# Mixture of experts on one core: eight experts gathered at once, and a scatter that takes one half of the tokens per expert pair

## The chip, the cores and the metric

The kernel runs on one core of a Trainium2 chip. The core has five engines, each with its own instruction queue: TensorE (PE, matmuls; its weight loads are listed as PEld), VectorE (DVE), ScalarE (ACT), GpSimd (POOL) and SyncE (SP, which here only issues loads). They wait for each other through semaphores. The metric is the device time of one execution in microseconds (us), the median of several.

## What is computed

Two transformer blocks over 256 tokens of width 1024, all in fp32. The change touches one stage of the first block, the mixture of 32 experts, each with 256 hidden columns; every token goes to two of them:

```python
def hier_moe(h, w_rg, b_rg, w_re, b_re, w_gate, w_up, w_down):
    ...
    x_pad = jnp.zeros((P, D), h.dtype).at[dest].set(xt[stok])
    ...
    def expert_block(args):
        xb, e = args
        hid = jax.nn.silu(xb @ w_gate[e]) * (xb @ w_up[e])
        return hid @ w_down[e]
    ...
    out = jnp.zeros((T, D), jnp.float32).at[tok_pad].add(y.astype(jnp.float32) * w_pad[:, None])
    return out.astype(h.dtype).reshape(B, L, D)
```

## The kernel before

**Slots.** The 256 tokens lie in two halves (tiles j = 0, 1) of 128. Each expert has CAP = 64 slots, CT = 32 for each half. DVE writes `Pm`, a 0/1 matrix with a column for each slot, by comparing each token's position with the slot numbers (`places`, L2509, L2511); `Pw` is the same with the router's weights (L2534). If an expert has over 32 tokens of a half, the branch `over > 0` runs further rounds; for the inputs measured it is not taken, but every engine has its code and jumps over it.

**Gather.** On PE, `gather` (L1673, L1678) multiplies the normalised tokens `xn2` by `Pm`: for a block of 128 model columns k, two matmuls, one for each half. A fill is two blocks, in PSUM bank 1 or 2; ACT scales it into `xgs` (`gathered`, L989, L995). Four experts (a quad, two pairs) are gathered at once, so a fill is 4 matmuls of 128 columns, and four fills make a quad. Four fills stand ahead of the loop; in each pair two more are made for the next quad, for the last quad too, whose fills nobody uses. There are 36 fills in all.

**A pair.** PE's loop (L1697) has 4 passes of 4 pairs. For each pair, in this order: gate and up into bank 0 (L1716, 32 matmuls, two experts side by side in 64 columns each; the two weight tiles of each come from `spare` or from the ring), a gather fill, `scatter` (L1687) of the pair before, transposes of the hidden rows and of `Pw` into bank 3 (L1727, L1728), a gather fill, and down into banks 1 and 2 (L1739). Beside it ACT makes silu (L1009), its gathered rows (L995) and the copy of the transposes `hT_PT` (L1012); DVE makes the hidden rows `hid` (L2544) and multiplies the result in banks 1 and 2 by the gate row into `ysb` (L2547), one copy of 128 partitions for each bank. Rows 0 to 63 of `ysb` belong to token half 0, rows 64 to 127 to half 1; the scatter is therefore 4 matmuls of 64 rows and 512 columns, into the four banks `acc`, where the sum over all experts stands. The first pair's scatter adds zeros; `last` (L1743) makes the one of pair 15.

**Waits.** PE's gather waits for `y_taken` (DVE's copies of the pair before), the transposes for `hid_ready`, down for `t_taken` (ACT's copy of the transposes), the first pair for the last of the gathered rows.

**Weights.** A pair takes 6 tiles of 1 MB. Pairs 0, 2, 4, ... read them from `spare`, the others from the ring; the first two pairs' tiles are there when the stage begins. SP then loads the tiles of pair n + 2 into the same places, in order: two when gate of pair n is done, two after up, two after down (L589 to L595). 84 tiles are loaded so.

## Time and profile before

| what | us |
|---|---|
| median of 3 runs (lowest, highest) | 1232.71 (1231.29, 1232.84) |
| the profiled execution, its own time | 1231.89 |
| its span | 1229.6 |
| PE busy in it | 1169.0 (95%) |
| DVE busy | 408.4 (33%) |
| ACT busy | 322.3 (26%) |
| MoE stage, first gather to last scatter | 540.6 to 790.6 |

The run fetched code by two queues, 0.70 MB and 0.15 MB, and executed 16523 instructions in the span.

The profile records one execution. All times in its rows are from the start of the span; the 2.3 us between the span and the execution's own time lie around it. A matmul in fp32 shows as two records, so the counts of PE rows are twice those of the code. PE's records overlap a little at their ends: the time from one start to the next says more than the duration.

### The profile page before, as it was taken

The page shows a single profiled execution, that of the slowest core. Times are in us where ns is not written, and L with a number is a line of the kernel's source. Part 1 is how long each engine was busy: PE and PEld are TensorE (multiplying, and loading weights), DVE is VectorE, ACT ScalarE, POOL GpSimd, SP SyncE. Part 2 cuts the span into 40 slices and gives each one's busy share as a digit, 9 for nine tenths or more (in the row PEclk, how much of TensorE's full clock was granted, in tenths as well). Part 3 has the DMA queues.
Part 4 walks back from the last instruction along what each step waited for, and adds up shares of the span by engine and source line. Part 5 has one row for each costly group of instructions (what it writes and reads, how often), then busy time and mean ns, then how long its engine had stood idle before and what let it go on. Part 6 is the DMA issues. An engine that isn't in the chain of part 4 may idle for free.

```text
span 1229.6 us, 16523 instructions
## 1 busy us (share of the span) xinstructions
PE 1169.0 (95%) x6732; PEld 868.1 (71%) x6732; DVE 408.4 (33%) x1006; ACT 322.3 (26%) x739; POOL 32.2 (3%) x56
## 2 busy tenths in 40 slices
PE   7999999999999999989999999889778989999997
PEld 6788888888887778865555555467656848887443
DVE  2324334213322131231111111125886432225445
ACT  3481010053423130141122211243475241000000
POOL 0000000000000002000000000014000000000000
PEclk9999999999999999999999999999879999999999
DMA  9923113212247784629999999523200413434430
GB/s 387 405 102 137 69 69 134 106 70 103 103 146 316 281 335 155 241 88 390 410 422 425 423 415 378 206 103 136 106 1 1 171 69 139 169 137 171 171 136 34
DMA packets 34153, 241.66 MB, mean 197 GB/s; under 512 B 3898, under 2 KB 4154, under 8 KB 5804
## 3 DMA queue, kind: packets, MB, share of 16 engines
q1 hardware_dynamic: 32940, 234.46, 48.7%
q0 software_dynamic: 720, 3.12, 0.7%
q10 hardware_dynamic: 432, 3.23, 0.6%
q8 instruction: 43, 0.70, 0.2%
q14 instruction: 18, 0.15, 0.0%
HBM read 239.74 MB, written 1.05 MB: 196 GB/s over the span
## 4 chain that ended last, share of the span: by engine, by line
PE 87%; DVE 6%; ACT 3%; DMA 2%; issue 1%; SPq 0%; DVEq 0%; ACTq 0%
PE bank L1318 22%; PE bank L1345 12%; PE bank L1716 9%; PE bank L1327 8%; PE bank L2066 6%; PE bank L1739 5%; PE bank L1678 3%; PE bank L1390 3%; PE bank L1687 3%; DMA ring<-in_stream 2%; PE bank L1410 1%; PE bank L1584 1%; PE bank L1581 1%; PE bank L1529 1%; PE bank L2038 1%
## 5 line engine op out<-in xcount | busy, mean ns | idle before, releaser
L1318 PE MATMUL bank<-arena,ring 128*128 128x256 f32 x736 | 159.3, 379 | 0.0
L1318 PEld LDWEIGHTS bank<-arena,ring 128*128 128x128 f32 x736 | 139.9, 190 | 18.8
L1318 PE MATMUL bank<-hTl,ring 128*128 128x256 f32 x512 | 112.8, 379 | 0.0
L1318 PEld LDWEIGHTS bank<-hTl,ring 128*128 128x128 f32 x512 | 97.1, 190 | 16.8 <-issue 4.3
L696 ACT ACTIVATE arena<-bank 128x512 f32<-128x512 f32 x70 | 41.2, 600 | 235.9 <-PE bank L1318 211.4
L1345 PE MATMUL bank<-ring,arena 128*128 128x256 f32 x432 | 95.9, 380 | 1.0 <-ACT arena L1177 0.7
L1345 PEld LDWEIGHTS bank<-ring,arena 128*128 128x128 f32 x432 | 81.9, 190 | 12.6 <-ACT arena L1177 1.0
L1327 PE MATMUL bank<-ring,arena 128*128 128x256 f32 x352 | 77.9, 380 | 1.2 <-DMA ring<-in_stream 1.2
L1327 PEld LDWEIGHTS bank<-ring,arena 128*128 128x128 f32 x352 | 66.5, 190 | 11.2 <-DMA ring<-in_stream 1.7
L1716 PE MATMUL bank<-ring,arena 128*64 128x256 f32 x512 | 57.0, 381 | 0.0
L1327 PE MATMUL bank<-ring,hTl 128*128 128x256 f32 x256 | 56.9, 380 | 0.0
L2547 DVE TENSOR_TENSOR arena<-bank,arena 128x512 f32<-128x512 f32 x32 | 22.1, 692 | 101.9 <-PE bank L1739 101.9
L1327 PEld LDWEIGHTS bank<-ring,hTl 128*128 128x128 f32 x256 | 48.4, 190 | 7.7 <-issue 1.3
L1716 PEld LDWEIGHTS bank<-ring,arena 128*64 128x64 f32 x512 | 36.1, 137 | 24.0 <-issue 6.7
L1009 ACT ACTIVATE arena<-bank 128x256 f32<-128x256 f32 x16 | 6.1, 383 | 151.8 <-PE bank L1716 151.8
L1390 PE MATMUL bank<-ring,arena 128*128 128x256 f32 x192 | 44.9, 390 | 0.2 <-ACT arena L952 0.2
L1678 PE MATMUL bank<-arena 128*128 128x128 f32 x288 | 41.1, 290 | 1.6 <-DVE arena L2511 1.6
L995 ACT ACTIVATE arena<-bank,mod 128x256 f32<-128x256 f32 x72 | 36.7, 560 | 21.0 <-PE bank L1678 20.9
L1678 PEld LDWEIGHTS bank<-arena 128*128 128x128 f32 x288 | 36.4, 199 | 8.0 <-issue 7.9
L1390 PEld LDWEIGHTS bank<-ring,arena 128*128 128x128 f32 x192 | 37.1, 197 | 6.0 <-issue 0.6
L2544 DVE TENSOR_TENSOR arena<-arena,bank 128x256 f32<-128x256 f32 x16 | 6.7, 421 | 101.9 <-ACT arena L1009 101.9
L809 ACT ACTIVATE arena<-bank 128x256 f32<-128x256 f32 x36 | 12.5, 382 | 90.6 <-PE bank L1345 90.6
(506 smaller groups left out, 1669.8 us busy)
## 6 DMA issues: line engine op xcount, KB each, us to landing
ring<-in_stream SPq DMA_DIRECT2D x163, 1024.0 KB, 6.9
arena<-in_stream SPq DMA_DIRECT2D x38, 1024.0 KB, 9.4
hTl<-in_stream SPq DMA_DIRECT2D x9, 1024.0 KB, 8.4
hTc<-in_stream SPq DMA_DIRECT2D x9, 1024.0 KB, 10.3
consts<-in_consts ACTq DMA_DIRECT2D x1, 3081.0 KB, 15.5
arena<-in_mem SPq DMA_DIRECT2D x1, 1024.0 KB, 5.8
arena<-in_x SPq DMA_DIRECT2D x1, 1024.0 KB, 18.8
arena<-in_ctx SPq DMA_DIRECT2D x1, 1024.0 KB, 20.8
```

Of the source, the lines that this page charges most:

```text
L696: act.activation(dst, b[:, :].rearrange("p (a b) -> p a b", b=two), func, scale=scale).then_inc(sum_taken, 1)
L995: ins = act.activation(xgs[q][:, k, :].rearrange("p (e j c) -> p j e c", e=4, j=NT), b[:, 256 * m:256 * m + 256].rearrange("p (j e c) -> p ...
L1318: mm = pe.matmul(b[:, 256 * n:256 * n + 256], w[:, k, 128 * n:128 * n + 128], h[:, k, :], start=(k == 0), stop=(k == KD - 1))
L1327: mm = pe.matmul(b[:, 256 * i:256 * i + 256], h[:, k, 128 * i:128 * i + 128], w[:, k, :], start=(k == 0), stop=(k == KD - 1))
L1345: mm = pe.matmul(b, lhs(*source, k), rhs[:, k, :], start=(start and k == 0), stop=(k == 3), skip_group_check=True)
L1390: mm = pe.matmul(b[:, 256 * i:256 * i + 256], h[:, k, 128 * i:128 * i + 128], w[:, k, :], start=(k == 0 and i == 0), stop=(k == KD - 1), s ...
L1678: mm = pe.matmul(bank[1 + fill % 2][:, at:at + 128], xn2[:, j, 128 * k:128 * k + 128], Pm[:, j, :], start=True, stop=True)
L1687: mm = pe.matmul(acc[2 * j + n][:, :], hT_PT[own, 256:384], ysb[own, 512 * n:512 * n + 512], start=False, stop=False, skip_group_check=True)
L1716: mm = pe.matmul(bank[0][CAP * e:CAP * e + CAP, FF * a:FF * a + FF], xgs[q][:, k, at:at + CAP], w[e][:, k, :], start=(k == 0), stop=(k == ...
L1739: mm = pe.matmul(bank[1 + m][to:to + CT, :], hT_PT[:, of:of + CT], wd[e][:, k, 512 * m:512 * m + 512], start=(k == 0), stop=(k == 1), skip ...
L2066: mm = pe.matmul(prod[m][:, :], lhs, rhs, start=(q == 0), stop=(q == 15))
L2547: dve.tensor_tensor(ysb[:, 512 * m:512 * m + 512], bank[1 + m][:, :], g2bc[:, 512 * m:512 * m + 512], ALU.mult).then_inc(R.y_taken, 1)
```

## The change

- **Eight experts at once.** `Pm` and `Pw` are twice as wide. A fill is now one block k, 2 matmuls of 256 columns in a whole bank; 8 fills make an octet (four pairs), 32 in all. Eight fills stand ahead of the first pair, two are made in each of pairs 0 to 11 for the next octet, none in pairs 12 to 15. ACT's `gathered` is one copy of 512 elements. The gathered rows of every second octet lie half in `FA` and half in `V + 2048`.
- **Scatter at full height.** The down matmuls of odd pairs write the two token halves in exchanged places (`j ^ n % 2`), and DVE copies each bank in two halves of 64 partitions to different buffers: the rows of token half 0 of pairs 2q and 2q + 1 meet in one buffer of 128 rows, those of half 1 in another (two of these, in the constants' `qdec`, no longer needed then). `scatter(j, quad)` is 2 matmuls of 128 rows and 512 columns for one token half and four experts. Pair n, from pair 2 on, makes the one of half n % 2 of the quad before; two stand after the last pair. `hT_PT` has two buffers.
- **No loop.** The 16 pairs are written out on PE, ACT and DVE; SP keeps its loop.

```diff
-                    for m in range(2):
-                        k = 2 * fill + m
-                        for j in range(NT):
-                            at = 256 * m + 128 * j
-                            mm = pe.matmul(bank[1 + fill % 2][:, at:at + 128], xn2[:, j, 128 * k:128 * k + 128],
-                                           Pm[:, j, :], start=True, stop=True)
+                def gather(k):
+                    for j in range(NT):
+                        mm = pe.matmul(bank[1 + k % 2][:, 256 * j:256 * j + 256], xn2[:, j, 128 * k:128 * k + 128],
+                                       Pm[:, j, :], start=True, stop=True)
+                    mm.then_inc(R.xg_ready, 1)
...
-                    for n in range(2):
-                        for j in range(NT):
-                            own = slice(2 * CT * j, 2 * CT * j + 2 * CT)
-                            mm = pe.matmul(acc[2 * j + n][:, :], hT_PT[own, 256:384], ysb[own, 512 * n:512 * n + 512],
-                                           start=False, stop=False, skip_group_check=True)
+                def scatter(j, quad):
+                    for n in range(2):
+                        mm = pe.matmul(acc[2 * j + n][:, :], hT_PT[j][:, 256:384],
+                                       expert_rows(j, quad)[:, 512 * n:512 * n + 512],
+                                       start=False, stop=False, skip_group_check=True)
...
+                    pe.wait_ge(R.y_taken, r * (2 * PAIRS + 2) + (2 * n + 2))
+                    if ahead:
+                        pe.wait_ge(R.p_ready, r * OCTS + (o + 2))
+                        gather(2 * h)
+                    if n >= 2:
+                        scatter(n % 2, n // 2 - 1)
+                    pe.wait_ge(R.hid_ready, r * (PAIRS + 1) + (n + 2))
+                    pe.wait_ge(R.pw_ready, r * OCTS + (o + 1))
+                    for f in range(2):
+                        pe.transpose(bank[3][:, 128 * f:128 * f + 128], hid[:, 128 * f:128 * f + 128], ident)
+                    pe.transpose(bank[3][:, 256:384], Pw[:, 128 * h:128 * h + 128], ident).then_inc(R.t_ready, 1)
+                    if ahead:
+                        gather(2 * h + 1)
+                    pe.wait_ge(R.t_taken, r * PAIRS + (n + 1))
...
-                    scatter().then_inc(R.added, 1)
+                    scatter(0, QUADS - 1)
+                    scatter(1, QUADS - 1).then_inc(R.added, 1)
...
-                            dve.tensor_tensor(ysb[:, 512 * m:512 * m + 512], bank[1 + m][:, :],
-                                              g2bc[:, 512 * m:512 * m + 512], ALU.mult).then_inc(R.y_taken, 1)
+                        for g in range(2):
+                            own = slice(64 * g, 64 * g + 64)
+                            ins = dve.tensor_tensor(expert_rows(g ^ n % 2, n // 2)[own, c], bank[1 + m][own, :],
+                                                    g2bc[own, c], ALU.mult)
+                        ins.then_inc(R.y_taken, 1)
```

How PE's rows stand in a pair in the middle of the stage. An x counts matmuls, the last size is that of the output (partitions, columns). Before, an odd pair from the gather to the first half of down:

```order
L1678 MATMUL bank<-arena 128x128 [waits moe_downs_taken,moe_places]
L1678 MATMUL bank<-arena 128x128 x3
L1687 MATMUL bank<-arena 128x512 x4
L1724 REGISTER_ALU
L1727 MATMUL bank<-consts,arena 128x128 [waits moe_weighted,moe_hidden]
L1727 MATMUL bank<-consts,arena 128x128
L1728 MATMUL bank<-consts,arena 128x128
L1678 MATMUL bank<-arena 128x128 x4
L1734 REGISTER_ALU [waits tile_loaded4,tile_loaded3,moe_turned_taken]
L1739 MATMUL bank<-ring,arena 32x512 [waits moe_gathered_taken]
L1739 MATMUL bank<-ring,arena 32x512 x7
```

After, the same piece of pair 3 (`moe_turned_taken` is `t_taken`, `moe_hidden` is `hid_ready`):

```order
L1685 MATMUL bank<-arena 128x256 [waits moe_places,moe_downs_taken]
L1685 MATMUL bank<-arena 128x256
L1692 MATMUL bank<-consts,arena 128x512 x2
L1736 MATMUL bank<-consts,arena 128x128 [waits moe_weighted,moe_hidden]
L1736 MATMUL bank<-consts,arena 128x128
L1737 MATMUL bank<-consts,arena 128x128
L1685 MATMUL bank<-arena 128x256 x2
L1750 MATMUL bank<-ring,arena 32x512 [waits tile_loaded4,moe_gathered_taken,tile_loaded3,moe_turned_taken]
L1750 MATMUL bank<-ring,arena 32x512 x7
```

Each gather is two wide matmuls instead of four, the scatter two instead of four, and the order of the steps stays.

PE after, in the first pair, between up and the transposes, where no scatter stands:

```order
L1723 MATMUL bank<-arena 64x256 [waits spare_loaded3,spare_loaded2]
L1723 MATMUL bank<-arena 64x256 x15
L1685 MATMUL bank<-arena 128x256 [waits moe_places,moe_downs_taken]
L1685 MATMUL bank<-arena 128x256
L1736 MATMUL bank<-consts,arena 128x128 [waits moe_weighted,moe_hidden]
```

One fill of two matmuls is all that lies between up and the wait for the hidden rows there. In pairs 12 to 15 it is the other way round: a scatter and no fill.

## Rows read from the trace of the kernel before

**Rows 1.** Page, chain that ended last, share of the span by engine

```profile
PE 87%; DVE 6%; ACT 3%; DMA 2%; issue 1%; SPq 0%; DVEq 0%; ACTq 0%
```

**Rows 2.** Timeline: start us, length us, engine, line, what, xcount, [idle before <-releaser]

```profile
562.65 7.13 PE L1716 MATMUL bank<-ring,arena 128*64 128x256 f32 x64
...
569.71 1.16 PE L1678 MATMUL bank<-arena 128*128 128x128 f32 x8
569.82 0.38 ACT L1009 ACTIVATE arena<-bank 128x256 f32<-128x256 f32 x1 [9.62 <-PE bank L1716]
570.31 0.42 DVE L2544 TENSOR_TENSOR arena<-arena,bank 128x256 f32<-128x256 f32 x1 [6.83 <-ACT arena L1009]
...
570.80 1.99 PE L1687 MATMUL bank<-arena 64*128 64x512 f32 x8
...
572.71 0.44 PE L1727 MATMUL bank<-consts,arena 128*128 128x128 f32 x2
...
573.10 1.06 PE L1678 MATMUL bank<-arena 128*128 128x128 f32 x8
573.30 0.49 ACT L1012 ACTIVATE arena<-bank 128x384 f32<-128x384 f32 x1 [1.37 <-PE bank L1728]
...
574.08 3.64 PE L1739 MATMUL bank<-ring,arena 128*32 128x512 f32 x32
...
607.66 0.43 PE L1716 MATMUL bank<-hTl,arena 128*64 128x256 f32 x1
```

**Rows 3.** Stretches: length, then PE, PEld, DVE, ACT, POOL busy, PEclk, DMA share, GB/s

```profile
592.60:607.60 15.00, 15.00 (x127) 8.35 (x123) 1.80 (x3) 2.91 (x6) 0.00 (x0) 1.00 0.99 405
...
667.60:682.60 15.00, 15.00 (x127) 8.36 (x123) 2.70 (x7) 2.91 (x6) 0.00 (x0) 1.00 1.01 426
```

**Rows 4.** Timeline, PE alone, full-height matmuls ahead of the stage

```profile
499.64 7.07 PE L1390 MATMUL bank<-ring,arena 128*128 128x256 f32 x32
506.54 7.07 PE L1327 MATMUL bank<-ring,arena 128*128 128x256 f32 x32
...
532.80 3.68 PE L1659 MATMUL bank<-arena,consts 128*128 128x512 f32 x8
```

**Rows 5.** Timeline of the stage's beginning, and a stretch of it (columns as above)

```profile
539.98 0.49 DVE L2511 TENSOR_TENSOR arena<-arena,consts 128x128 f32<-128x128 f32 x2
...
540.62 5.63 PE L1678 MATMUL bank<-arena 128*128 128x128 f32 x32 [1.63 <-DVE arena L2511]
...
545.20 2.10 ACT L995 ACTIVATE arena<-bank,mod 128x256 f32<-128x256 f32 x4 [0.17 <-PE bank L1678]
...
547.65 0.40 PE L1716 MATMUL bank<-hTl,arena 128*64 128x256 f32 x1 [1.40 <-ACT arena L995]
...
543.20:544.10 0.90, 0.90 (x6) 0.90 (x6) 0.00 (x0) 0.21 (x2) 0.00 (x0) 0.50 0.00 0
```

**Rows 6.** Groups by line: xcount | busy us, mean ns | idle before, releaser

```profile
L696 ACT ACTIVATE arena<-bank 128x512 f32<-128x512 f32 x70 | 41.2, 600 | 235.9 <-PE bank L1318 211.4
...
L809 ACT ACTIVATE arena<-bank 128x256 f32<-128x256 f32 x36 | 12.5, 382 | 90.6 <-PE bank L1345 90.6
```

**Rows 7.** Chain in order of time at the stage's end: start, us, what

```profile
787.86 0.70 DVE arena L2547
...
788.60 2.01 PE bank L1687 x8
...
791.94 3.48 issue
```

**Rows 8.** First load of the stage (timeline), stretch in which the last lands

```profile
551.52 0.35 SPq L595 DMA_DIRECT2D hTl<-in_stream  x1
...
766.00:768.00 2.00, 2.00 (x10) 0.77 (x11) 0.00 (x0) 0.98 (x2) 0.00 (x0) 1.00 0.06 25
```

**Rows 9.** A stretch of straight code early in the kernel; queue that fetches code

```profile
31.00:61.00 30.00, 28.23 (x211) 21.26 (x210) 10.21 (x22) 12.11 (x26) 1.82 (x3) 1.00 1.01 405
...
q8 instruction: 43, 0.70, 0.2%
```

More of the change, by code:

```diff
@@ L27 @@
 QUADS = PAIRS // 2
+OCTS = PAIRS // 4
 MOE_RING = 3 * EXPERTS // 2
@@ L1001, in experts @@
-                fills = 2 * PAIRS + 4
-                for f in range(4):
-                    gathered(0, f, r * fills + (f + 1))
-                with act.Fori(0, QUADS // 2) as i:
-                    for n in range(4):
-                        q, h = divmod(n, 2)
-                        act.wait_ge(R.u_done, r * PAIRS + (i * 4 + (n + 1 + R.ahead)))
-                        act.wait_ge(R.hid_ready, r * (PAIRS + 1) + (i * 4 + (n + 1)))
-                        act.activation(sil, bank[0][:, 0:FF], ACT.Silu).then_inc(R.sil_ready, 1)
-                        gathered(1 - q, 2 * h, r * fills + (i * 8 + (2 * n + 5)))
-                        act.wait_ge(R.t_ready, r * PAIRS + (i * 4 + (n + 1)))
-                        act.activation(hT_PT, bank[3][:, 0:384], ACT.Copy).then_inc(R.t_taken, 1)
-                        gathered(1 - q, 2 * h + 1, r * fills + (i * 8 + (2 * n + 6)))
+                fills = KD * OCTS
@@ new lines, in gathered @@
+                def gathered(o, k):
+                    act.wait_ge(R.xg_ready, r * fills + (KD * o + k + 1))
+                    act.activation(gathered_rows(o, k).rearrange("p (e j c) -> p j e c", e=8, j=NT),
+                                   bank[1 + k % 2][:, :].rearrange("p (j e c) -> p j e c", e=8, j=NT),
+                                   ACT.Identity, bias=mod2[:, k:k + 1], scale=mod2[:, 8 + k:9 + k]).then_inc(R.xg_taken, 1)
+                for k in range(KD):
+                    gathered(0, k)
@@ new lines, in experts @@
+                for n in range(PAIRS):
+                    o, h = divmod(n, 4)
+                    act.wait_ge(R.u_done, r * PAIRS + (n + 1 + R.ahead))
+                    act.wait_ge(R.hid_ready, r * (PAIRS + 1) + (n + 1))
+                    act.activation(sil, bank[0][:, 0:FF], ACT.Silu).then_inc(R.sil_ready, 1)
+                    if o + 1 < OCTS:
+                        gathered(o + 1, 2 * h)
+                    act.wait_ge(R.t_ready, r * PAIRS + (n + 1))
+                    act.activation(hT_PT[n % 2], bank[3][:, 0:384], ACT.Copy).then_inc(R.t_taken, 1)
+                    if o + 1 < OCTS:
+                        gathered(o + 1, 2 * h + 1)
@@ new lines, in experts @@
+                for n in range(PAIRS):
+                    o, h = divmod(n, 4)
+                    if h == 0:
+                        for j in range(NT):
+                            to = Pw.rearrange("p (q j h x) -> p j q h x", q=2, j=NT, h=2)[:, j, :, :, :]
+                            of = of_tile(j).rearrange("p (q h e) c -> p q h e c", q=2, h=2)
+                            by = per_expert(cw, j, o).rearrange("p (q h e) c -> p q h e c", q=2, h=2)
+                            for half in range(2):
+                                ins = dve.tensor_tensor(to[:, :, half ^ j, :].rearrange("p q (e c) -> p q e c", e=2),
+                                                        of[:, :, half, :, :], by[:, :, half, :, :], ALU.mult)
+                        ins.then_inc(R.pw_ready, 1)
+                        if o + 1 < OCTS:
+                            dve.wait_ge(R.pw_ready, r * OCTS + (o + 1))
+                            dve.wait_ge(R.xg_taken, r * (KD * OCTS) + KD * (o + 1))
+                            places(o + 1)
+                    dve.wait_ge(R.u_done, r * PAIRS + (n + 1 + R.ahead))
+                    dve.wait_ge(R.sil_ready, r * PAIRS + (n + 1))
+                    dve.tensor_tensor(hid, sil, bank[0][:, FF:2 * FF], ALU.mult).then_inc(R.hid_ready, 1)
+                    for m in range(2):
+                        dve.wait_ge(R.y_ready, r * (2 * PAIRS) + (2 * n + m + 1 + 2 * R.ahead))
+                        c = slice(512 * m, 512 * m + 512)
+                        for g in range(2):
[3 more added lines that the diff above has]
+                        ins.then_inc(R.y_taken, 1)
```

164 lines of the change are left out of this document (64 added, 100 removed).

## Prediction

> **What bounds the kernel now.** I read the chain that ended last first [rows 1]: 87% of the span is TensorE (PE), so a microsecond taken from PE's own work is a microsecond off the time, unless something else becomes late. Next comes the timeline of one expert pair, the unit that the change rewrites [rows 2]. Its PE rows follow each other without a hole: gate and up 562.65 to 569.71 (7.06 us), one gather to 570.80 (1.09), the scatter to 572.71 (1.91), transposes to 573.10 (0.39), the other gather to 574.08 (0.98), down to the next pair (3.57). The first pair starts at 547.65, the fifth at 607.66: 60.01 for four, 15.00 each, and the sixteen take 240.0 us, to 787.65. PE is busy for all of it. The third thing is the weight traffic beside it: 405 GB/s at a DMA share of 0.99, later 426 at 1.01 [rows 3]. So two resources are full at once, and the saving on PE counts only as far as the loads keep up.
>
> A record is half of an fp32 matmul (32 gate and up matmuls show as 64), so each 128-column gather fill of 4 matmuls is 8 records, and the new one of 2 matmuls is 4 records of 256 columns.
>
> **Prices on PE.** Full-height records of 256 columns start 6.90 us apart per 32 (499.64 to 506.54), 0.216 us each. Full height with 512 columns: 8 in 3.68, of which the tail of the last is about 0.2, so 0.435 each; twice 0.216 is 0.43 [rows 4].
>
> **Gathers inside the pairs.** Now 16 records of 128 columns cost 1.09 + 0.98 = 2.07 per pair, in all 16 pairs. After it is 8 x 0.216 = 1.73, in pairs 0 to 11 alone: 0.34 off each of twelve, 2.07 off each of the last four.
>
> **Scatters.** Eight half-height records of 512 columns took 1.91, or 0.24 each, although one of that width costs 0.435 alone: the two halves of the rows already run beside each other [rows 2, 4]. The new scatter has 4 full-height records, 4 x 0.435 = 1.74, 0.17 off. So "full height" buys nearly nothing per pair; what it does is drop the scatter from pairs 0 and 1 (the old pair 0 scattered zeros) and put two at the end. The Trainium skill, "TensorE: Matmul & The Clock Gate", section "Why this matters for your kernels", says the same against this edit: a matmul of few rows lasts as long as one of 128, and the gain of small ones is that tiles in distinct row groups run concurrently. By that rule alone the gain per scatter would be 0; by the rows it is 0.17.
>
> **Stalls that the cover leaves bare.** Two waits stand behind work that goes. First, the transposes need the hidden rows, ready at 570.31 + 0.42 = 570.73, seen at 570.80, which is 1.09 after gate and up. In pairs 0 and 1 only a gather of 0.86 covers that: 0.23 of stall. From pair 2 on gather or scatter covers it. Second, down needs ACT's copy of the transposes: started 573.30, 0.49 long, so usable about 573.85, 0.75 after the transposes end [rows 2]. A gather of 0.86 covers it in pairs 0 to 11, by 0.1; in the last four nothing does: 0.75 each.
>
> **Sum of the pairs.** Pairs 0, 1: 15.00 - 1.91 - 0.34 + 0.23 = 12.98, twice. Pairs 2 to 11: 15.00 - 0.34 - 0.17 = 14.49, ten. Pairs 12 to 15: 15.00 - 2.07 - 0.17 + 0.75 = 13.51, four. Together 224.9 against 240.0: 15.1 off.
>
> **Before the first pair.** Eight fills instead of four stand there. The clock was 0.50, the lower of the two levels, while the first fills ran; I count the first two at 1.7 us each, since 5.63 for four leaves this when the last two cost 1.1, and a new fill has as many columns. The other six at 4 x 0.216: 5.2. That is 8.6 against 5.6, +3.0. The two place comparisons double in width: 0.49 becomes twice 0.42 [rows 2, 5], +0.35. The last ACT copy is one of 512 elements instead of two of 256 (2.10 for four, 0.51 each); the step from 256 to 512 elements costs 600 - 382 = 0.22 [rows 6], so 0.73, which shortens the end by 0.25. If ACT's time grows with the elements, to 1.02, ACT sets the pace of these fills and 1.3 us more are due. Taken: 0.73, as the contiguous rows are nearest. Sum +3.1, up to +4.4.
>
> **Copies of the expert rows.** DVE does four of 64 partitions where two of 128 took 0.70. No row shows a 64-partition copy; between 0.35 and 0.70 I take 0.70, since width along the row is unchanged and that sets all the prices I have. Within the pairs the cover is gate and up, 7.06 us, against at most 1.4 of copies; at the first pair of an eight, another 1 us of weights and 0.85 of places: 3.3, still covered. At the end it is bare: one more copy before the last scatter, +0.70. The last scatter is 8 records of 0.435 plus 0.15, 3.6, instead of 2.01 [rows 7]: +1.6. Together +2.3. The 3.48 us of "issue" after it, where PE jumps over the unused overflow branch, stays; the jump is longer, but was not free before.
>
> **Sum.** -15.1 + 3.1 + 2.3 = -9.7. The profiled execution's span of 1229.6 becomes 1219.9, its own time of 1231.89 becomes 1222.2, and the median of 1232.71, 0.8 above it, 1223.0.
>
> **Do the loads keep up?** 84 tiles are loaded during the pairs, the first issued at 551.52, 3.9 after pair 0 starts, the last landed about 766.1 [rows 8]. Less some 1.5 us without work early on, that is 213 us, 2.52 per tile, when nothing waited for them. After: they end near 3.9 + 213 = 217 after pair 0 starts. Pair 15 starts at 211.4 and needs its up weights at 214.9; these are two tiles from the end, 212. Its down weights it needs at 221.3. So 3 us are left, where before it was 15 (761 against 776.2). I take no wait. The Trainium skill, "HBM Reference", section "Specifications (TRN2)", gives about 358 GB/s as a core's share and 425 for one streaming alone; by 358 the 88 MB would take 246 us and the change would be lost. The trace differs: this core already draws 426 [rows 3].
>
> **Rivals.**
> A, the loads bind. If the mean is the 405 GB/s of an early stretch and not 417, the last tile lands 6 later and the up weights 3 late: 1226. At 398 it is 1229. For it: both resources run full, and the unrolled loop adds code traffic. Against: the backlog grew by little in 13 pairs. 0.14.
> B, slower: fetching the code. The loop ran from the same code four times; unrolled, PE reads every pair afresh, through DMA engines that are full. Code comes in pieces of 16.3 KB (43 packets, 0.70 MB [rows 9]). The run read 0.85 MB for the some 13,200 of its 16,523 instructions that are not repeats of the loop, 64 bytes each, and a pair has 250 on PE: one piece per pair. If each comes late by x, 15 of them cost 15x; it decides from x = 0.65. At 1 us each it is 1238. Against it stands 31 to 61 us [rows 9]: straight code, 421 records in 30 us, DMA share 1.01, and PE busy 28.23. That is 14 a microsecond; the pairs need 16. 0.09.
> C, more gain: the seams between groups (7.06 for 64 records of which two run side by side) shrink without loop registers, or the half copies cost 0.35: 2 to 3 us more, 1220.5. 0.08.
> D, the loop itself. The Trainium skill, "Runtime: NRT & Kernel Launch", section "Instruction fetch mechanics", says that a taken branch out of the fetched window stalls the engine and that kernels prefer full unrolling. Here three jumps back go; at the 3.48 of [rows 7] each that would be 10 us more, 1213. But the pair after a jump began on time, 60.01 after four [rows 2, 5]. 0.01.
>
> **How the numbers follow.** The forecast, 1223.0, has 0.68, with 1220.5 to 1225.5 for its own unknowns (the ACT copy +1.3, the half copy -0.7, prices of 0.43 or 0.44). The range must take in A and C and leaves out B's far part: 1219.5 to 1228.5. Within 0.2%, about 2.5 us and what a measurement of this kernel can tell, is 1230.2 to 1235.2. Faster than that: the forecast, C, D and 0.11 of A, 0.88. Same: the far end of A and a mild B, 0.05. Slower: B, 0.07.
>
> **What would show it.** In the new timeline: pairs 2 to 11 at 14.5, 12 to 15 at 13.5 with 0.75 of PE idle put down to ACT's copy; first pair about 3.1 later; last scatter 3.6. A shows as PE waits put down to a DMA in pairs 14 and 15. B shows as idle "issue" on PE inside pairs, spaced by one pair or so. A DVE copy of 0.35 would show in the groups by shape.

## The result, and where the time went

The changed kernel takes 1221.8 us, the median of 4 runs (1218.28 to 1224.36), beside 1232.78 for the kernel before on the same chip: a ratio of 0.9908 with a 95% interval of 0.9879 to 0.9937. The forecast was 1223.0. The profiled execution took 1218.28, its span is 1216.0 instead of 1229.6. It is the fastest of these four executions, so of the 13.6 us between the two spans only about 11 are in the medians.

The spans are split at three points that each trace shows: the first places comparison on DVE, the first matmul of pair 0, the end of the last scatter. The ends of PE's records are modelled, so in every kernel I take the end of the last scatter as the start of its last record plus 0.43 us, the price of such a record; the chain rows have it 0.16 to 0.18 later.

| stretch, us | before | after | difference | forecast |
|---|---|---|---|---|
| start to first places | 539.98 | 539.01 | -1.0 | 0 |
| first places to pair 0 | 7.67 | 11.15 | +3.5 | +3.1 |
| pairs 0 to 15 | 240.1 | 226.2 | -13.9 | -15.1 |
| end of pair 15 to end of last scatter | 2.7 | 5.1 | +2.4 | +2.3 |
| the stage (the three above) | 250.45 | 242.48 | -8.0 | -9.7 |
| last scatter to the end | 439.18 | 434.53 | -4.7 | 0 |

So the stage gave 1.7 us less than forecast, and a stretch in which the change edits nothing gave 4.7 more.

The pairs first. Timeline of the kernel after, PE and ACT in pair 3, which answers to [rows 2] (start us, length us, engine, line, what, xcount):

```profile
612.55 1.13 PE L1685 MATMUL bank<-arena 128*128 128x256 f32 x4
613.52 1.88 PE L1692 MATMUL bank<-arena 128*128 128x512 f32 x4
...
615.23 0.38 PE L1736 MATMUL bank<-consts,arena 128*128 128x128 f32 x2
...
615.56 1.03 PE L1685 MATMUL bank<-arena 128*128 128x256 f32 x4
...
616.52 3.64 PE L1750 MATMUL bank<-arena 128*32 128x512 f32 x32
```

From start to start: a fill 0.97, the scatter 1.71, transposes 0.33, the other fill 0.96, and gate, up and down unchanged at 7.06 and 3.57. That is 14.60 in each of pairs 2 to 11, where before it was 15.00. Pairs 0 and 1 take 13.08 and 13.05, pairs 12 to 14 take 13.52 each.

The same pair, and one further on, in stretches (columns as in [rows 3]):

```profile
605.49:620.09 14.60, 14.60 (x115) 7.92 (x111) 4.84 (x11) 2.43 (x4) 0.00 (x0) 1.00 1.01 425
...
735.00:749.60 14.60, 14.02 (x118) 6.71 (x108) 3.94 (x7) 0.88 (x2) 0.00 (x0) 1.00 1.01 425
```

The first has no idle PE. In the second, among the last four pairs, PE misses 0.58 us, and the loads still draw 425 GB/s. PE's waits from 540 to 784 us, in groups (what waited, for what, us in total, times, longest):

```profile
PE bank L1750 <- ACT arena L1020: 2.3, 4, 0.6
PE bank L1685 <- DVE arena L2524: 1.9, 1, 1.9
PE bank L1692 <- DVE arena L2564: 1.5, 1, 1.5
PE bank L1723 <- ACT arena L1006: 0.9, 1, 0.9
```

The first line is the predicted stall in pairs 12 to 15, four times 0.58. This is PE's idle time after the modelled end of the last transpose record; from start to start the step from the transposes to down takes 1.07 us there (771.72 to 772.79 in pair 15), of which the transposes need 0.33, so that 0.74 are lost. No line names a DMA. Code fetches by queue q8 grew from 0.70 MB [rows 9] to 0.88 MB. The page's group for the new copies:

```profile
L2564 DVE TENSOR_TENSOR arena<-bank,arena 64x512 f32<-64x512 f32 x32 | 22.0, 689 | 38.6 <-PE bank L1750 38.3
```

The half copy of 64 partitions takes 0.69 us, as much as the whole one of 128 did [rows 7].

The beginning of the stage after, timeline, and a stretch of it, which answer to [rows 5]:

```profile
539.01 0.76 DVE L2524 TENSOR_TENSOR arena<-arena,consts 128x256 f32<-128x256 f32 x2
...
539.92 9.38 PE L1685 MATMUL bank<-arena 128*128 128x256 f32 x32 [1.91 <-DVE arena L2524]
...
541.27 0.78 ACT L1006 ACTIVATE arena<-bank,mod 128x512 f32<-128x512 f32 x1 [2.36 <-PE bank L1685]
...
546.47 1.64 ACT L1006 ACTIVATE arena<-bank,mod 128x512 f32<-128x512 f32 x2 [0.36 <-PE bank L1685]
...
550.16 0.43 PE L1723 MATMUL bank<-hTl,arena 128*64 128x256 f32 x1 [0.87 <-ACT arena L1006]
...
540.80:541.20 0.40, 0.40 (x3) 0.31 (x2) 0.22 (x2) 0.00 (x0) 0.00 (x0) 0.50 0.00 0
```

ACT's copies come two in every 2.00 us (1.64 of work and 0.36 of waiting for PE), each fill needing one of only two banks back. So the fills that run at the upper clock are paced at 1.0 us by PE and ACT together, not at the 0.86 of PE alone. The first ones run at the lower clock (0.50).

The end of the stage after, chain in order of time, answers to [rows 7]:

```profile
777.95 3.71 PE bank L1692 x8
781.66 2.01 issue
783.68 0.70 DVE arena L2579
784.38 0.46 issue
784.84 1.94 PE bank L1386 x16
```

Before, the same 16 matmuls came 4.99 us after the last scatter and took 3.65 us; now they come after 3.36 us and take 1.94. Their row in the kernel before, then PE's own row for the jump over the overflow branch, before and after (PEldq is the sequencer that feeds PE; then count, ns min/median/max, first and last start):

```profile
795.42 3.65 PE bank L1377 x16
...
L1755 PEldq COMPARE_BRANCH  x1: 6633/6633/6633, 788.6 to 788.6; - x1
...
L1768 PEldq COMPARE_BRANCH  x1: 6713/6713/6713, 778.0 to 778.0; - x1
```

In both kernels the jump begins with the first matmul of the last scatter (788.60 and 777.95) and lasts 6.6 to 6.7 us, and PE's next matmul comes 0.2 us behind it. The last scatter now takes 3.54 us instead of 1.83, so it covers 1.7 us more of the same jump. That is the shorter gap: the longer last scatter, which costs 1.7 us in the stage, costs nothing in the sum as long as the jump stands there.

Over the 415 to 420 us behind the last scatter the difference can be read from one stretch of each kernel (length, PE busy with its records, and so on; the clock's mean is before the DMA share). Before, then after:

```profile
790.43:1210.00 419.57, 384.17 (x1929) 280.03 (x1928) 200.55 (x564) 112.28 (x318) 19.12 (x19) 0.96 0.32 115
```

```profile
781.49:1196.40 414.91, 381.63 (x1928) 277.79 (x1928) 200.64 (x564) 112.35 (x318) 19.14 (x19) 0.97 0.32 114
```

Both stretches have the same work in them, 1928 weight loads and as many matmuls, with one more cut by the window's edge before. Of the 4.7 us, 2.5 are PE's busy time at another mean clock, 1.6 are the shorter gap behind the scatter, 0.5 other idle time. By the clock records of the two traces, 36.6 us behind the last scatter ran at the lower level before and 26.8 us after.

### The profile page after: what moved, and what is told of

Same layout as the page of the kernel before. It is cut to its first block, busy times and chain, and to the rows that moved or that the text cites. A ratio compares the mean times of both kernels' runs of the same rounds, so it can differ in the third digit from the quotient of the medians.

```text
span 1216.0 us, 15813 instructions
## 1 busy us (share of the span) xinstructions
PE 1155.4 (95%) x6500; PEld 852.4 (70%) x6500; DVE 429.0 (35%) x1028; ACT 310.4 (26%) x699; POOL 32.3 (3%) x56
## 4 chain that ended last, share of the span: by engine, by line
PE 87%; DVE 6%; ACT 3%; DMA 2%; issue 1%; SPq 0%; DVEq 0%; ACTq 0%
PE bank L1327 22%; PE bank L1354 12%; PE bank L1723 9%; PE bank L1336 9%; PE bank L2079 6%; PE bank L1750 5%; PE bank L1399 3%; PE bank L1685 3%; PE bank L1692 2%; DMA ring<-in_stream 2%; PE bank L1419 1%; PE bank L1593 1%; PE bank L1590 1%; PE bank L1538 1%; PE bank L2051 1%; PE bank L2094 1%
## 5 line engine op out<-in xcount | busy, mean ns | idle before, releaser
L3019 DVE TENSOR_TENSOR arena<-arena 128x512 f32<-128x512 f32 x16 | 11.1, 693 | 75.7 <-ACT arena L708 75.7
L1685 PE MATMUL bank<-arena 128*128 128x256 f32 x128 | 35.3, 407 | 1.9 <-DVE arena L2524 1.9
L2564 DVE TENSOR_TENSOR consts<-bank,arena 64x512 f32<-64x512 f32 x32 | 22.0, 689 | 38.6 <-PE bank L1750 38.4
L2564 DVE TENSOR_TENSOR arena<-bank,arena 64x512 f32<-64x512 f32 x32 | 22.0, 689 | 38.6 <-PE bank L1750 38.3
```

The lines of the kernel that those rows point to most:

```text
L1685: mm = pe.matmul(bank[1 + k % 2][:, 256 * j:256 * j + 256], xn2[:, j, 128 * k:128 * k + 128], Pm[:, j, :], start=True, stop=True)
L2564: ins = dve.tensor_tensor(expert_rows(g ^ n % 2, n // 2)[own, c], bank[1 + m][own, :], g2bc[own, c], ALU.mult)
```

## The experiments

All ratios are to the kernel before, run beside it on the same chip.

### The same kernel again, and the loop alone

`changed_again` has no edit: it asks whether the 4.7 us behind the stage come back.

> The changed kernel a second time. The first profile ended 3.9 us earlier than the sum said, although its expert stage saved less than the sum (pairs at 14.60 and 13.1 where 14.49 and 12.98 were forecast). The rest lay after the stage: PE waited 3.2 us there instead of 4.8 and its clock stayed at the upper level for the next matmuls (1.94 us instead of 3.65). Theory: that part comes from the jump over the overflow branch and differs from run to run; then this profile need not show it, and the median stays near 1222. Rival: it belongs to the changed code; then this profile shows 3.2 and 1.94 again. The stage itself should read the same to 0.2 us: pairs 2 to 11 at 14.60, 12 to 15 at 13.51, last scatter 3.7.

Median 1220.68, ratio 0.9908 (0.9894 to 0.9923). Its stage takes 242.47 us, each pair agrees within 0.05 us, and behind the scatter it takes 434.43. The profile shows both parts of the gain again. But it is the fastest of its four executions (1218.14, the others 1220.47 to 1220.98), as the first one was of its own. The two medians of the first result lie some 2.6 us less apart than the two profiled spans, and no trace shows in which stretch the other executions are longer; the 4.7 us may be smaller in them.

`unrolled` is the kernel before with its pairs written out:

```diff
-                with pe.Fori(0, QUADS // 2) as i:
+                for i in range(QUADS // 2):
```

and so on ACT and DVE. Gather and scatter are as before.

> The kernel before with nothing changed but the loop of the expert stage, written out on PE, ACT and DVE (16 pairs). Theory: neither the jumps back nor the fetch of straight code cost anything, so pairs stay at 15.00 and the time at 1232.7, within 1 us. Rival (jumps back stall): three of them go, up to 10 us less, 1223. Rival (code fetch through full DMA engines): idle 'issue' on PE about once a pair, 1240 or more.

Median 1231.14 of 12 runs, ratio 0.9997 (0.9987 to 1.0008). Every pair takes 15.00 us. Its timeline, a gather fill and the one of the next pair:

```profile
598.36 1.16 PE L1678 MATMUL bank<-arena 128*128 128x128 f32 x8
...
613.36 1.16 PE L1678 MATMUL bank<-arena 128*128 128x128 f32 x8
```

No idle "issue" stands on PE inside the pairs. Writing out the loop neither costs (rival B) nor gains (rival D). Its profiled span is 2.9 us shorter than before: 1.4 ahead of pair 0, since the lower clock fell on work ahead of the first fills (places to pair 0 in 6.06 instead of 7.67), and 1.5 behind the last scatter.

### The halves of the change

`half_scatter` keeps the gather of eight and takes the old scatter back:

```diff
-                    if n >= 2:
-                        scatter(n % 2, n // 2 - 1)
+                    scatter()
...
-                        for g in range(2):
...
+                        dve.tensor_tensor(ysb[:, 512 * m:512 * m + 512], bank[1 + m][:, :],
+                                          g2bc[:, 512 * m:512 * m + 512], ALU.mult).then_inc(R.y_taken, 1)
```

> The changed kernel with the scatter of before: four matmuls of 64 rows in every pair (zeros in pair 0), one copy of 128 partitions for each bank, one scatter after the last pair; eight experts gathered at once, no loop. Theory: the two halves of the rows already ran side by side, so a scatter costs 1.91 against 1.72 (0.19 x 14 = 2.7), pairs 0 and 1 get one of 1.91 each in place of 0.3 of stall (+3.1), and the end gets one copy and half a scatter less (-2.4): 3.4 us slower than the changed kernel, 1225. Rival (full height halves the scatter's work): 14 x 1.9 us more, 1248. Rival (the scatter's part is nothing): 1222.

Median 1228.56 of 10 runs, ratio 0.9971 (0.9962 to 0.998). Pairs 0 to 11 take 14.95, pairs 12 to 14 take 13.67. PE in one pair, from the timeline:

```profile
601.98 1.13 PE L1686 MATMUL bank<-arena 128*128 128x256 f32 x4
603.04 1.99 PE L1695 MATMUL bank<-arena 64*128 64x512 f32 x8
...
605.35 1.03 PE L1686 MATMUL bank<-arena 128*128 128x256 f32 x4
606.30 3.64 PE L1751 MATMUL bank<-ring,arena 128*32 128x512 f32 x32
```

The fill between up and a half-height scatter takes 1.06, the scatter 1.92 (to the transposes at 604.96), the second fill 0.95. The new gather is worth 0.05 us per pair beside the old scatter; the new scatter is worth another 0.35 (14.95 to 14.60), more than the 0.17 at which it was priced. From pair 0 to the end of the last scatter the run takes 236.8 us, 5.5 more than the changed kernel; the whole run was expected to be 3.4 slower, with 0.19 for each of 14 pairs, and its median is 7.9 above that of `changed_again`. The gather's larger use is that it needs no fills in the last four pairs.

Where the 0.35 lie is seen in single records. PE in the kernel before, the last three twos of half-height records and what follows; then in the changed kernel the last full-height one and what follows (timelines of windows that hold these alone):

```profile
571.33 0.59 PE L1687 MATMUL bank<-arena 64*128 64x512 f32 x2
...
571.76 0.59 PE L1687 MATMUL bank<-arena 64*128 64x512 f32 x2
...
572.19 0.60 PE L1687 MATMUL bank<-arena 64*128 64x512 f32 x2
...
572.71 0.44 PE L1727 MATMUL bank<-consts,arena 128*128 128x128 f32 x2
```

```profile
629.40 0.59 PE L1692 MATMUL bank<-consts,arena 128*128 128x512 f32 x1
...
629.83 0.38 PE L1736 MATMUL bank<-consts,arena 128*128 128x128 f32 x2
```

Two half-height records that start together last as long as one at full height: the next two start 0.43 later, just as the next full-height one does. So the work in the scatter is the same. But the first step of the half-height group takes 0.53 (570.80 to 571.33) and the last, up to the transposes, 0.52 (572.19 to 572.71), where inside the group and at full height it is 0.43. The fill ahead is 0.09 longer and the transposes behind 0.06. I call these the seams of the group: a matmul group between groups of another tile height or width takes about 0.1 us more at each of its ends, and so do its neighbours. The full-height scatter has the shape of the fills and transposes around it and no such seam. What in the engine makes them no run shows.

`idle_fills` is the changed kernel with the eight fills back in pairs 12 to 15, whose rows nobody uses:

```diff
-                    ahead = o + 1 < OCTS
+                    ahead = True
```

> The changed kernel with two gather fills in pairs 12 to 15 as well, as the kernel before makes them for nobody (rows written to the free buffer, not read). Theory: those pairs go from 13.51 to 14.60, because a fill costs 1.73 and takes 0.63 of bare wait for ACT's copy away: 4.4 us slower than the changed kernel, 1226. Rival (the fills only fill time in which PE waits anyway): no difference, 1222. Rival (loads bind when pairs are short, so shorter pairs gave nothing): no difference either, but with PE waits on a DMA in the changed kernel, which its first profile does not show.

Median 1228.74 of 9 runs, ratio 0.9971 (0.9959 to 0.9984). The last pairs take 14.60 like the others, the stage 246.79, 4.3 more than in the changed kernel. So leaving out the fills gives 1.08 in each of the four pairs, not the 1.93 that they cost: the wait for ACT's copy takes 0.74 back, and the scatter, now directly behind up, takes 1.82 from start to start (769.90 to 771.72 in the changed kernel) instead of 1.71. The span grew by 11.2, of which 6.6 lie behind the last scatter. Part of those is a hole inside a group that is otherwise without one, with the lower clock from 790.3 to 797.1 us:

```profile
789.47 1.85 PE L1384 MATMUL bank<-consts,arena 128*128 128x128 f32 x11 [3.23 <-DVE arena L2578]
792.31 1.23 PE L1384 MATMUL bank<-consts,arena 128*128 128x128 f32 x5 [0.99 <-issue]
```

### What moves behind the stage

`before_no_branch` and `changed_no_branch` leave out the branch `over > 0`, the load of its flag and its code on every engine, so that an overflowing expert would go uncomputed; for the inputs measured only the flag's load and the jump are gone:

```diff
-            pe.wait_ge(over_ready, 1)
-            over = pe.value_load(over_i[0:1, 0:1], min_val=0, max_val=1)
...
-            with pe.If(over > 0):
-
-                for s_ in (more.g_done, more.u_done, more.y_ready, more.y_ready) * 2:
-                    pe.matmul(bank[3][0:1, 0:2], ident[:, 0:1], ident[:, 0:2], start=True, stop=True).then_inc(s_, 1)
-                with pe.Fori(0, L // CAP - 1) as r:
-                    experts(more, r, more_loaded, more_spare, lambda s: 16)()
```

> The kernel before without the overflow branch: its rounds, the load of its flag and the waits for it are left out on all engines. Its two profiles so far (as it was, and with its loop written out) show 5.0 and 4.5 us from the last scatter to the next matmul, of which the two DVE copies need 1.4, and then a stretch at the lower clock that falls on the next matmuls. Theory (the jump over unread code holds PE back): 1.4 us there, so 3.6 less, and up to 2 us more if the clock stays up: 1226 to 1228 against 1231.6. Rival (something else makes that gap): 5.0 again, 1231.6.

> The changed kernel without the overflow branch. Two profiles show 3.3 us from the last scatter to the next matmul, here because DVE begins its copies 2.0 us late. Theory: 1.4 us, so 2 us less, 1219 against 1220.7 to 1221.8. Together with the same cut in the kernel before it tells what the change is worth without the branch: the stages differ by 8.0 us in the profiles, so by theory the two kernels without a branch differ by 8 us and a rest that only the places of the low-clock stretches make. Rival (the 4.7 us that the kernel after gained behind the stage belongs to the change itself): they differ by 11 to 13 us still.

Medians 1225.33 and 1218.02, ratios 0.9945 (0.9925 to 0.9965) and 0.988 (0.9862 to 0.9897). The chain in order of time at the stage's end, of before without the branch, then of after without it:

```profile
788.06 2.01 PE bank L1663 x8
...
790.84 1.97 PE bank L1353 x16
```

```profile
780.26 3.71 PE bank L1668 x8
...
784.75 1.97 PE bank L1362 x16
```

The gap is 0.95 us in both, most of it one copy of 0.70 us on DVE. And the stretches behind the last scatter, in the same order:

```profile
789.89:1204.20 414.31, 380.83 (x1929) 277.05 (x1928) 200.67 (x564) 112.55 (x318) 19.10 (x19) 0.97 0.33 116
```

```profile
783.80:1198.10 414.30, 380.90 (x1928) 277.08 (x1928) 200.65 (x564) 112.55 (x318) 19.13 (x19) 0.97 0.33 114
```

PE's busy time agrees within 0.1 us, and the whole rest is 433.88 and 433.93. The lower level holds for 27.5 and 27.4 us of it. So the 4.7 us belong to the branch and to the clock behind it. The two runs take out the flag's load together with the jump; the trace tells them apart, as on PE the load is over before the last scatter starts and the jump alone spans 6.6 us. With the branch gone the change is worth 7.75 us in the stage (250.28 to 242.53) and 7.3 in the medians. The branch, jumped over, costs the kernel before 7.3 us of its median (1232.61 to 1225.33, by the interval 4.3 to 9.2); 5.3 of it stand behind the last scatter in the profiles. The changed kernel pays some 3 in the medians, which the intervals hardly tell from nothing (0.9894 to 0.9923 with the branch, 0.9862 to 0.9897 without), and 0.6 behind the last scatter in the profiles.

### The fills ahead of pair 0

`kept_busy` puts seven matmuls whose result is not used ahead of the first gather, in the time in which PE waits for the places:

```diff
+            def busy(k):
+                for _ in range(k):
+                    pe.matmul(bank[1][:, 0:256], ident, xn2[:, 0, 0:256], start=True, stop=True)
```

> The changed kernel with seven matmuls of 256 columns more, whose results nobody reads, in the two holes of PE ahead of the stage (four before the rank sums, three after). Theory: the clock is at its lower level for the first two fills only because PE stood idle before them; kept busy it stays up, the first two fills take 0.9 instead of 1.7 each, and from the places to the first pair it is 9.5 us instead of 11.1 (ACT's copies then pace the fills): 1.5 us less, 1219.5. Rival (the lower stretch comes whether PE is busy or not): it takes 11.1 again and nothing is gained; worse by up to 0.5 if the matmuls are in the way.

The eight fills in its timeline, which took 9.38 in the changed kernel, and the clock during them:

```profile
543.05 7.97 PE L1694 MATMUL bank<-arena 128*128 128x256 f32 x32 [0.56 <-DVE arena L2533]
...
543.90:544.30 0.40, 0.40 (x4) 0.35 (x3) 0.26 (x2) 0.11 (x1) 0.00 (x0) 1.00 0.00 0
```

From the places to pair 0 it is 9.74 instead of 11.15, the stage is 241.07. The twelve profiles without these matmuls all have a stretch at the lower clock between 531 and 546 us; this one and `short_end_busy`, the two with them, have none from 450 to 785 us. So here it hung on PE's idle time ahead of the fills. The extra matmuls are not the only way to 9.74, though: in `half_scatter`, `extra_quarter` and `extra_eighth` it is 9.74 as well, because the stretch fell ahead of the places.

In the profiled execution the gain was lost elsewhere: the places came 3.1 us later than in the changed kernel, a stretch at the lower clock fell on the matmuls behind the stage, and the rest took 438.58. That execution is the slowest of the four (1224.10; the others 1218.3 to 1221.8), so the loss may be smaller in the others. The median is 1220.26, ratio 0.99 (0.9882 to 0.9918): the same as the changed kernel's.

### How much room the loads have

`extra_quarter` and `extra_eighth` load 0.26 and 0.13 MB more in each pair from the third on, 14 times, into places that nobody reads; SP's loop is written out:

```diff
+                        if s == 2:
+                            if count >= 3:
+                                sp.wait_ge(extra_in, 16 * (count - 2))
+                            sp.dma_start(region(QK + 2560 + 512 * (count % 3), 512), stream[0][:, 0:512]).then_inc(extra_in, 16)
+                            count += 1
```

> The changed kernel with one load of 0.26 MB more per pair, fourteen in all, into a place that nobody reads (SP's loop is written out for it). At 425 GB/s they need 8.6 us. Theory (the loads have 5 us left: in the first profile the last tile landed about 766.5, two tiles earlier 761.5, and pair 15 needed its up weights at 766.4): PE waits for loads in the last pairs, 8.6 - 5 = 3.6 us, 1225. Rival (the loads bound the changed kernel already, so that every microsecond of load shows): 8.6 us more, 1230. Rival (the loads are far from the bound): nothing, 1221.

> The changed kernel with 0.13 MB more loaded for each pair from the third on (14 loads, nobody reads them), where the earlier run loaded 0.26 MB more and lost 3.7 us in the stage. Its 1.8 MB are 4.3 us at 425 GB/s. If 3 us are left, as the prediction has it, 1.3 us are lost; if 5 are left, as the last tiles' landing in the changed kernel says, nothing is lost and the stage takes 242.5. Rival (the loads already bind, every byte more costs time): 4.3 us lost.

In both, the lower clock missed the first fills (places to pair 0 in 9.74), so I compare from pair 0 to the end of the last scatter, which is 231.33 in the changed kernel. With the quarter it is 236.47, 5.1 more; pairs 13 and 14 take 15.15 and 15.12 instead of 13.52. With the eighth it is 231.87, 0.5 more. PE's waits on a DMA, of the quarter, then of the eighth:

```profile
PE bank L1730 <- DMA ring<-in_stream: 3.1, 2, 1.7
...
PE bank L1730 <- DMA arena<-in_stream: 1.4, 1, 1.4
```

```profile
PE bank L1730 <- DMA ring<-in_stream: 0.3, 1, 0.3
```

At 425 GB/s the added bytes are 8.6 and 4.3 us. Less 5.1 and 0.5 this leaves 3.5 and 3.8 us of room, by two runs. The 5 us that I had read from the landing of the last tiles were too many; the prediction's 3 were nearer. The medians are 1226.63, ratio 0.9958 (0.9942 to 0.9975), and 1220.51, ratio 0.9914 (0.9896 to 0.9932).

### Another order for the last four pairs

`short_end` moves parts of the scatter of pairs 12 to 15 behind the transposes and scatters the last quad at half height, one pair after the other:

```diff
-                    if n >= 2:
+                    if n in (PAIRS - 3, PAIRS - 1):
+                        scatter(1, n // 2 - 1, (1,))
+                    elif n >= 2:
...
+                    if n == PAIRS - 1:
+                        scatter_pair(hT_PT[0], first_rows, (0,))
...
+                    if n in (PAIRS - 4, PAIRS - 2):
+                        scatter(1, n // 2 - 1, (0,))
+                    if n == PAIRS - 1:
+                        scatter_pair(hT_PT[0], first_rows, (1,))
...
-                    scatter(0, QUADS - 1)
-                    scatter(1, QUADS - 1).then_inc(R.added, 1)
+                    scatter_pair(hT_PT[1], second_rows[:, 1, :], (0, 1)).then_inc(R.added, 1)
```

`short_end_busy` adds the seven matmuls of `kept_busy`, `short_end_no_branch` leaves out the branch.

> The changed kernel with another order of its last four pairs. In pairs 12 to 15 a half of the scatter (one matmul of 128 rows, 0.86 us) stands behind the transposes, so that ACT's copy of them (PE's wait of 0.6 us in each of these pairs) is covered. The last quad is scattered at half height, pair 14's part inside pair 15 and pair 15's behind it, with DVE's copies of 128 partitions as before the change. Sum from rows: four waits of 0.6 less (-2.4), the last DVE copies one of 0.70 instead of two of 0.69 (-0.7), the last scatter 1.9 instead of 3.4 (-1.5), pair 14's own scatter inside pair 15 (+1.9), some seams (+0.6): -2.1. My theory (PE's own rows and waits set these pairs): the stage from the first places to the last scatter's end takes 240.4 us, against 242.5. Rival (the loads bind in the last pairs, in which 3 to 5 us are left, or the wait only moves to the hidden rows): under 1 us less, and a PE wait on DMA or on DVE in these pairs. The median also depends on where the jump over the branch and the low-clock stretches fall behind the stage, up to 5 us either way.

> The same with seven matmuls whose result is not used ahead of the first gather, while PE waits for the places, as in the run with these matmuls alone, which brought the stage from 242.5 to 241.1. My theory (the two effects lie at the two ends of the stage and add): the stage takes 239.0 us. Rival (they don't add, since the loads then bind): 240 or more, with waits on DMA in the last pairs. Behind the stage I can't say where the low clock falls; the run with these matmuls alone lost there what it won here.

> The short end, with the branch over > 0 and its code left out on all engines, so that what follows the stage can be compared with the two kernels without a branch (433.9 us from the last scatter to the end in both). My theory (behind the stage only the jump and the clock differ between these kernels): the stage 240.4, the rest 433.9, and about 2.1 us less than the changed kernel without the branch. Rival (the rest depends on the stage's last engines' timing in another way): a rest that differs by over 1 us from 433.9 with the low-clock stretches in the same places.

Three of the four waits went, not four as I had written. Pair 13 has nothing behind its transposes, and PE's groups of waits from 740 us on show that one, with the wait for the last copy, now 0.8 instead of 1.5:

```profile
PE bank L1702 <- DVE consts L2589: 0.8, 1, 0.8
PE bank L1767 <- ACT arena L1020: 0.6, 1, 0.6
```

From pair 0 to the end of the last scatter each of the three kernels takes 229.41 us, against 231.33: 1.9 us less, three times. The stages are 240.8, 239.2 and 240.6, where 240.4, 239.0 and 240.4 were expected. In the medians nothing of it can be told: 1222.17, ratio 0.9937 (0.9922 to 0.9952); 1224.24, ratio 0.9951 (0.9936 to 0.9965); 1217.09, ratio 0.9894 (0.9875 to 0.9913). With the branch, the chain behind the shortened stage reads:

```profile
780.39 4.76 issue
785.15 0.70 DVE arena L2608
...
785.90 3.67 PE bank L1386 x16
```

The next matmuls come 5.7 us after the last scatter, which is short again (1.83 us), and meet the lower clock, as in the kernel before; the rest takes 439.6. PE's jump, 6.19 us long, is over at 784.6 there, and what comes last is DVE, whose copy starts only at 785.15. Without the branch it takes 432.4 and not the 433.9 that I expected. PE's busy time there is 378.94 instead of 380.90, at a mean clock one hundredth higher (this stretch starts 0.16 us later than the others; with them it would be 379.1):

```profile
781.33:1194.00 412.67, 378.94 (x1927) 275.59 (x1928) 200.59 (x564) 112.33 (x318) 19.13 (x19) 0.98 0.33 117
```

The lower level holds for 22.9 us of the rest, instead of 27.4. Where the clock falls moved the rest by 1.5 us even without the branch. So I have no version that is shown to be better than the changed kernel with its branch.

## Why the prediction was right

**The bound.** That PE sets the stage held: in the changed kernel its waits inside the pairs are the predicted ones for ACT's copy, and none is for a DMA. Only the two runs with added loads have waits on a DMA.

**Pairs 2 to 11: 14.49 forecast, 14.60 measured.** The term that was mis-sized is "Gathers inside the pairs", where the new gathers were counted at 8 x 0.216 = 1.73. They take 0.97 + 0.96 = 1.93. The old ones had been read from start to start, 1.09 + 0.98, with the seams at both ends in them, the new ones priced from the inside of a long group of like matmuls [rows 4]. In ten pairs that is 2.0 us less gain. Beside the old scatter the new fills take 1.06 + 0.95 = 2.01, so wider matmuls alone gave 0.06 of the 0.34; another 0.08 came when the scatter next to them got their shape, and 0.20 of seams stayed. The scatter gave 0.20, forecast 0.17, and the transposes behind it 0.06, forecast nothing; together the miss is 0.11 per pair.

**The scatter.** Priced at 0.17, measured 0.20 in its own rows and 0.35 for the whole pair against `half_scatter`, since the fill ahead is also 0.09 shorter and the transposes behind 0.06. So inside the pairs the scatter gave the larger part, small as it is, and the 0.17 was near for a reason that the working did not have: it set 1.91 with seams against 1.74 without and took the difference for one of work. By the rule of the Trainium skill ("TensorE: Matmul & The Clock Gate", "Why this matters for your kernels") the gain would have been 0. For the matmuls themselves the trace agrees with the rule: two half-height records together are followed after 0.43 us, as one at full height is. The gain is that two changes of shape are gone.

**Pairs 0, 1 and 12 to 15.** Forecast 12.98 and 13.51, measured 13.08 and 13.05, and 13.52. In the last four the wait for ACT's copy is the forecast one, 0.74 from start to start instead of 0.75. The scatter takes 1.82 instead of 1.74 where no fill stands before it, and the transposes 0.33 instead of 0.39; these two nearly cancel. `idle_fills` confirms the sum of it, 1.08 per pair.

**Before the first pair: +3.1 forecast, +3.5 measured.** The single ACT copy took 0.78, forecast 0.73. That ACT and PE together pace the fills at 1.0 us was seen only as the case in which ACT takes 1.02; it came already at 0.78, as each fill waits for its bank. `kept_busy` and the three runs in which the lower clock fell elsewhere, 9.74 us each, show that 1.4 of the 11.15 us are the lower clock.

**The end: +2.3 forecast, +2.4 measured.** The half copy at 0.69 and the last scatter at 3.71 (3.6 forecast) are as priced from the nearest rows. But the 1.7 us of the longer scatter did not reach the sum, as the jump that began with it took as long as before.

**Rivals.** B and D fell with `unrolled`. A did not come, and the two runs with extra loads put the room at 3.5 to 3.8 us where the working had 3 (its 2.52 us per tile should be 2.54, from 213 us for 84 tiles, which changes nothing). C did not come: the copies cost 0.69, and of the seams only those at the scatter went.

**The 3.48 us of "issue" "stays".** This step was wrong, and in the helpful direction. It put the 3.48 behind the last scatter, while the jump runs beside the scatter from its first matmul on; a scatter longer by 1.7 us left 1.6 less to wait. The rest of what changed there, 2.5 us of PE's busy time and 0.5 of idle time, goes with the place of the lower clock, which the change moved without editing anything there.

**The sum, and luck.** For the profiled execution 1222.2 was forecast and 1218.28 measured: 1.7 us more than forecast in the stage, 4.7 less behind it and 1.0 less ahead of it, neither foreseen. The median was put 0.8 above the profiled execution and lies 3.5 above it. So the median of 1221.8 is 1.2 us from the forecast because misses of opposite sign met; right is the mechanism in the stage, with 8.0 of 9.7 us. Why the jump takes 5.1 to 7.1 us on PE, by kernel, and why the clock drops in one place rather than another, stays open.

## What to carry to other kernels

Price the old and the new form of a step in the same way, both from start to start in their place or both from the inside of a long group; a short group of matmuls between groups of another tile shape costs 0.1 us or so more at each end, and keeping neighbouring groups in one shape saved more here than making the matmuls wider. Ask what runs beside a step that grows: the longer last scatter was hidden by a jump that began with it. A change that shifts a stage by some microseconds can move what stands behind it by half of what it saves (4.7 beside 8.0 us), so read each stretch's own length before believing a total, and leave out the suspected cause in both kernels to compare. When work is removed, look at what it covered: here four pairs without fills kept 1.08 us of 1.93 each.

## What the runs showed of the hardware

- A branch that is jumped over cost 7.3 us in the kernel before and about 3 in the changed one. The jump takes PE 6.63 and 6.71 us by its own row (5.05 to 7.13 over the eleven profiles with it) and begins with the first matmul of the last scatter; what the scatter does not cover is a gap, 4.99 and 3.36 us against 0.95 without the branch. In the kernel before, the matmuls after the gap met the lower clock (16 of them in 3.65 us, 1.94 at the upper clock). A loop's jump back cost nothing that 12 runs could show; PE's rows for them have 0.08 to 0.24 us.
- Two half-height fp32 records of 512 columns (64 rows each) that start together are followed after 0.43 us, as one of 128 rows is. A group whose tile shape differs from its neighbours' takes about 0.1 us more at each end: steps of 0.53 and 0.52 instead of 0.43, a fill of 0.96 to 1.06 instead of 0.86.
- A DVE copy of 64 partitions and 512 columns out of PSUM takes 0.69 us, the one of 128 partitions 0.70.
- The mean granted clock behind the stage was 0.96, 0.97 or 0.98 by kernel, and PE's busy time for the same 1927 to 1929 records 384.2, 381.6, 380.8 or 378.9 us. The lower level held for 36.6, 26.8, 27.5 and 22.9 us of it. Keeping PE busy ahead of the fills took the lower clock away from them (1.4 us), and the median stayed the same.
- One core drew 425 GB/s over the pairs at a DMA share of 1.01, and extra bytes cost time only beyond the 3.5 to 3.8 us of room.
